# Expert weights in pair slots: 4 MB loads with 32 KB rows for gate and up, and the down biases moved to the last group

## What is computed

```python
def moe_ffn(h, w_router, b_router, w_e_gate, b_e_gate, w_e_up, b_e_up, w_e_down, b_e_down):
    ...
    def expert_step(acc, args):
        wg, bg, wu, bu, wd, bd, cw = args
        g = jnp.minimum(xt @ wg + bg, SWIGLU_LIMIT)
        u = jnp.clip(xt @ wu + bu, -SWIGLU_LIMIT, SWIGLU_LIMIT)
        y = ((u + 1.0) * g * jax.nn.sigmoid(SWIGLU_ALPHA * g)) @ wd + bd
        return acc + cw[:, None].astype(y.dtype) * y, None
```

## Time and profile before

| what | value |
|---|---|
| median of 3 runs | 1139.85 us |
| profiled execution, its own time | 1138.89 us |
| its span (first to last instruction) | 1137.1 us |
| TensorE matmul busy | 1092.3 us, 96% |
| VectorE, ScalarE, GpSimd busy | 409.6, 179.3, 90.3 us |
| share of the 16 DMA engines of the weights' queue | 93.1% of the span |
| moved | 438.88 MB, mean 386 GB/s |

### The profile page before, as it was taken

How to read it: one execution, slowest core, us unless ns; L and a number is a source line. 1 busy time by engine, 2 the same in 40 slices (tenths; PEclk the granted TensorE clock), 3 DMA queues, 4 the chain that set the end, 5 groups by cost and what they waited for, 6 DMA issues and landing times.

```text
span 1137.1 us, 14543 instructions
## 1 busy us (share of the span) xinstructions
PE 1092.3 (96%) x5733; PEld 513.9 (45%) x5733; DVE 409.6 (36%) x973; ACT 179.3 (16%) x370; POOL 90.3 (8%) x89
## 2 busy tenths in 40 slices
PE   8999999999999999999999999999999999999997
PEld 7888899843333333333333333333333333333333
DVE  5883666532223222223322222222222222222222
ACT  6546664400000000000000000000000000000000
POOL 2226447000000000000000000000000000000000
PEclk9999999999989999999999999999999999999999
DMA  9955724999999999999999999999999999999996
GB/s 309 344 195 220 225 75 147 425 405 421 428 418 412 427 429 428 427 429 428 429 428 429 428 429 427 429 428 429 429 428 429 426 429 427 430 427 428 426 428 280
DMA packets 50572, 438.88 MB, mean 386 GB/s; under 512 B 6786, under 2 KB 12998, under 8 KB 25062
## 3 DMA queue, kind: packets, MB, share of 16 engines
q1 hardware_dynamic: 50470, 438.23, 93.1%
q10 hardware_dynamic: 64, 0.14, 0.0%
HBM read 437.30 MB, written 1.05 MB: 385 GB/s over the span
## 4 chain that ended last, share of the span: by engine, by line
PE 65%; DMA 34%; issue 0%; DVE 0%; ACT 0%; POOL 0%; POOLq 0%; SPq 0%; DVEq 0%
PE bank L1939 35%; DMA ring<-in_w_e_up_dram 18%; DMA ring<-in_w_e_gate_dram 12%; PE bank L1912 3%; PE bank L1960 3%; DMA ring<-in_w_e_down_dram 3%; PE bank L1928 2%; PE bank L1533 2%; PE bank L1701 1%; PE bank L1702 1%; PE bank L1703 1%; PE bank L1980 1%; PE bank L1542 1%; PE bank L1544 1%; PE bank L1543 1%; PE bank L1536 1%
## 5 line engine op out<-in xcount | busy, mean ns | idle before, releaser
L1939 PE MATMUL bank<-ring,heads 128*64 128x512 f32 x3004 | 679.0, 599 | 14.8 <-DMA ring<-in_w_e_gate_dram 13.1
L1939 PEld LDWEIGHTS bank<-ring,heads 128*64 128x64 f32 x3004 | 204.2, 137 | 421.0 <-issue 376.5
L1463 DVE TENSOR_TENSOR x<-x,bank 128x512 f32<-128x512 f32 x124 | 79.8, 684 | 144.9 <-PE bank L1960 144.9
L1411 DVE TENSOR_SCALAR heads<-bank 128x512 f32<-128x512 f32 x32 | 22.1, 691 | 289.5 <-PE bank L1939 289.5
L907 ACT ACTIVATE work<-bank 128x256 f32<-128x256 f32 x32 | 12.3, 383 | 492.3 <-PE bank L1973 492.3
L708 POOL TENSOR_TENSOR x<-x,heads 128x256 f32<-128x256 f32 x2 | 1.4, 729 | 912.1 <-ACT heads L941 912.1
L1960 PE MATMUL bank<-heads,work 64*128 64x512 f32 x248 | 72.3, 641 | 0.0
L409 POOL TENSOR_TENSOR w_lo<-ring,w_hi 128x1024 fp32r<-128x1024 f32 (+1 forms) x35 | 65.3, 1894 | 53.8 <-ACT w_hi L731 53.8
L731 ACT ACTIVATE w_hi<-ring 128x512 fp32r<-128x512 f32 (+2 forms) x82 | 57.6, 732 | 25.2 <-PE bank L1790 7.3
L1912 PE MATMUL bank<-work,xn 128*128 128x128 f32 x480 | 58.5, 275 | 0.0
L1912 PEld LDWEIGHTS bank<-work,xn 128*128 128x128 f32 x480 | 56.0, 192 | 0.0
(11 more groups left out here) (323 smaller groups left out, 976.3 us busy)
## 6 DMA issues: line engine op xcount, KB each, us to landing
ring<-in_w_e_gate_dram SPq DMA_DIRECT2D x61, 2048.0 KB, 30.6
ring<-in_w_e_up_dram SPq DMA_DIRECT2D x61, 2048.0 KB, 31.7
ring<-in_w_e_down_dram SPq DMA_DIRECT2D x60, 2048.0 KB, 31.8
ring<-in_w_in_dram SPq DMA_DIRECT2D x8, 2048.0 KB, 10.2
ring<-in_w_e_down_dram SPq DMA_DIRECT2D x8, 1024.0 KB, 17.5
spare<-in_w_e_gate_dram SPq DMA_DIRECT2D x2, 2048.0 KB, 15.7
ring<-in_w_out_dram SPq DMA_DIRECT2D x2, 2048.0 KB, 8.1
ring<-in_w_e_up_dram SPq DMA_DIRECT2D x4, 1024.0 KB, 7.1
```

The source lines that it names most:

```text
L1411: nc.vector.tensor_scalar(e_g, banks[1][:, :], LIMIT, None, ALU.min).then_inc(g_made, 1)
L1463: ins = nc.vector.tensor_tensor(x[:, t, 512 * h:512 * h + 512], x[:, t, 512 * h:512 * h + 512], bank67[:, j % 2, :], ALU.add)
L1939: last = mm(bank[C * half:C * half + C, :], lhs(kk), kept_row[half] if kept else w[:, k, 512 * half:512 * half + 512], start=(kk == 0 and ...
```

## The change

- `ring` becomes four pair slots of 4 MB (`PAIR_ORDER`, `slots_of`); matrix n of the order takes pair n mod 4. The order of a step is gate(e), down(e - 1), up(e): `place_of` gives 3e - 1, 3e, 3e + 1.
- Gate and up weights are laid out so that partition p holds rows 8p to 8p + 7: as one load of 4 MB, 32 KB in one piece a partition (`load_matrix`). Halves of gate and up then are 16 KB pieces at a step of 32 KB. Down keeps its layout. `xn`, `gain_m` follow the new layout.
- Gate and up of experts 4 to 27 come by `load_matrix`, issued when the pair's last user is done as a whole; both halves of `product` wait for the whole. All else (experts 0 to 3, every down, the last group) comes by halves. In the loop the two halves of down are issued together.
- `spare` is filled by one load instead of two. The loads of the head and of experts 1 to 3 are written out in `first_experts`.
- TensorE: gate 0, gate 1, down 0, down 1, up 0, up 1. In even steps the gather stands before gate 0. The first scatter stands inside up 0, after its second k. VectorE's `keep_x` of even steps goes ahead of `keep_hT`.
- The down biases are no longer added at the step of expert 3, but in the last group: for column half 0 in the step of expert 28, for half 1 in that of expert 29 (`biased_half = u`).

The diff, cut to its core (the helpers that count semaphore values, `adds` and `count_at`, and the last expert's index changes are left out):

```diff
 RING = (3, 4, 5)
-EX_ORDER = (7, 3, 6, 4, 5, 0, 1, 2)
-EX_SLOTS = len(EX_ORDER)
...
+        def place_of(m, u):
+
+            return {"gate": 3 * u - 1, "up": 3 * u + 1, "down": 3 * u + 3}[m]
+        LAST_PLACE = {("up", STEPS - 1): 9, ("down", STEPS - 2): 10, ("down", STEPS - 1): 11}
+        def slots_of(n):
+            pair = PAIR_ORDER[n % len(PAIR_ORDER)]
+            return 2 * pair, 2 * pair + 1
+
...
                 src = a[ex_src[m]][0, bass.ds(e, 1)] if not isinstance(e, int) else a[ex_src[m]][0, e:e + 1]
-                return src.rearrange("o (h p k) n -> h p (o k n)", h=2, p=P)[h]
-
-            def load_half(m, h, e, place):
-
-                s = EX_ORDER[place % EX_SLOTS]
+                if m == "down":
+                    return src.rearrange("o (h p k) n -> h p (o k n)", h=2, p=P)[h]
...
+            def load_matrix(m, e, n):
+
+                s = slots_of(n)[0]
+                src = a[ex_src[m]][0, bass.ds(e, 1)].rearrange("o (p k) n -> p (o k n)", p=P)
+                sp.dma_start(ring[:, s:s + 2, :].rearrange("p s n -> p (s n)"), src).then_inc(ring_in[s], 16)
+
...
+            def first_experts():
+
+                def as_freed(m, e, of, done):
+
+                    for h in range(2):
+                        sp.wait_ge((half_done, mat_done)[h][of], done)
+                        load_half(m, h, e, place_of(m, e))
+                sp.wait_ge(*low_done(OUT))
+                load_half("gate", 1, 1, place_of("gate", 1))
+                sp.wait_ge(y_made, KD)
+                load_half("gate", 0, 0, 0)
+                sp.wait_ge(*low_done(OUT + 3))
+                sp.wait_ge(*low_done(OUT + 4))
+                load_half("up", 0, 0, place_of("up", 0))
+                sp.wait_ge(*low_done(OUT + 7))
+                sp.wait_ge(*low_done(OUT + 8))
+                load_half("up", 1, 0, place_of("up", 0))
+                load_by_halves()
+                load_half("gate", 0, 1, place_of("gate", 1))
+                for i in range(len(INTO_USED)):
+                    load_as_used(i)
+                sp.wait_ge(mat_done["up"], 1)
+                load_half("gate", 1, 2, place_of("gate", 2))
+                as_freed("down", 1, "gate", 2)
+                as_freed("up", 2, "down", 1)
+                as_freed("gate", 3, "up", 2)
+                as_freed("down", 2, "gate", 3)
+                as_freed("up", 3, "down", 2)
+
+            def expert_body(base, u, last=False):
+
+                it = base + u
+                ends = last and u == STEPS - 1
+                e = sp.snap(sp.to_reg(it & (E - 1)), min_val=0, max_val=E - 1)
+                e_before = sp.snap(sp.to_reg((it - 1) & (E - 1)), min_val=0, max_val=E - 1)
+                now, prev = sp.to_reg(it), sp.to_reg(it - 1)
+                if last:
+                    if u:
+                        for h in range(2):
+                            sp.wait_ge((half_done, mat_done)[h]["up"], prev)
+                            load_half("gate", h, e, place_of("gate", u))
+                    if ends:
+                        n = LAST_PLACE["up", u]
+                        s = slots_of(n)[1]
+                        sp.wait_ge(half_done["gate"], now)
+                        load_half("up", 0, E - 1, n)
+                        sp.wait_ge(mat_done["gate"], now)
+                        sp.dma_start(ring[:, s, 0:1024 * 3], source("up", 1, E - 1)[:, 0:1024 * 3]).then_inc(ring_in[s], 16)
+                        for h in range(2):
+                            sp.wait_ge((half_done, mat_done)[h]["down"], prev)
+                            load_half("down", h, e_before, LAST_PLACE["down", u - 1])
+                        return
+                    for h in range(2):
+                        sp.wait_ge((half_done, mat_done)[h]["gate"], now)
+                        load_half("down", h, e_before, place_of("down", u - 1))
+                    for h in range(2):
+                        sp.wait_ge((half_done, mat_done)[h]["down"], prev)
+                        load_half("up", h, e, place_of("up", u))
+                    return
+                sp.wait_ge(mat_done["up"], prev)
+                load_matrix("gate", e, place_of("gate", u))
+                sp.wait_ge(mat_done["gate"], now)
                 for h in range(2):
+                    load_half("down", h, e_before, place_of("down", u - 1))
+                sp.wait_ge(mat_done["down"], prev)
+                load_matrix("up", e, place_of("up", u))
...
@@ -1388,9 +1422,11 @@
                 rcols = rv[:, it:it + 4, :] if isinstance(it, int) else rv[:, bass.ds(it, 4), :]
                 chain(nc.vector.tensor_copy(now.rearrange("p (s j) -> p s j", j=4), rcols))
 
+                if not first and u % 2 == 0:
+                    keep_x(it, u)
                 if not first:
                     keep_hT(it)
-                if not first and not ends:
+                if u % 2 and not ends:
                     keep_x(it, u)
                 if u % 2 == 0:
                     for t in range(NT):
...
+            def product(m, h, bank, lhs, it, base, u, first=False, in_last=False, between=None):
+
+                n = 0 if first and m == "gate" else place_of(m, u)
+                if in_last:
+                    n = LAST_PLACE.get((m, u), n)
...
+                    s = slots_of(n)[h]
+                    halves = isinstance(base, int) or m == "down" or in_last
+                    by = h if halves else 0
+                    pe.wait_ge(ring_in[slots_of(n)[by]], count_at(n, by, base, in_last))
                     w = ring[:, s, :].rearrange("p (k n) -> p k n", k=4)
                 if h == 0 and m != "down" and not (first and m == "gate"):
...
+                    if between and k == 2:
+                        between()
...
+            def scatter(i, t, biased_half=None):
+
+                if biased_half == 0 and t == 0:
...
                         pe.wait_ge(added, i * 2 + h + 1)
+                    biases = h == biased_half
                     if biases:
...
             def expert(base, u, in_last=False):
 
                 it = base + u
+                biased_half = u if in_last else None
                 if u % 2 == 0:
                     pe.wait_ge(ex_made, it - 1)
+                    gather(None, 1, False)
                 pe.wait_ge(g_made, it)
                 product("gate", 0, banks[1], x_of(u), it, base, u, False, in_last)
                 turn_h(it)
-                if u % 2 == 0:
-                    gather(None, 1, False)
-                elif u % 2:
+                if u % 2:
                     gather(it + 3, 0, True)
                 turn_hot(it)
+                if u % 2 == 0:
+                    pe.wait_ge(ex_made, it)
+                product("gate", 1, banks[1], x_of(u), it, base, u, False, in_last)
                 pe.wait_ge(ehT_made, it)
                 product("down", 0, banks[3], h_of, it - 1, base, u - 1, False, in_last)
                 product("down", 1, banks[3], h_of, it - 1, base, u - 1, False, in_last)
-                if u % 2 == 0:
-                    pe.wait_ge(ex_made, it)
-                product("gate", 1, banks[1], x_of(u), it, base, u, False, in_last)
-                scatter(it - 1, 0, isinstance(it, int) and it == 3)
-                product("up", 0, banks[2], x_of(u), it, base, u, False, in_last)
-                scatter(it - 1, 1, isinstance(it, int) and it == 3)
+                product("up", 0, banks[2], x_of(u), it, base, u, False, in_last,
+                        lambda: scatter(it - 1, 0, biased_half))
+                scatter(it - 1, 1, biased_half)
                 product("up", 1, banks[2], x_of(u), it, base, u, False, in_last)
 
```

More of the change, by code:

```diff
@@ L414, in wait_block, with adds, count_at @@
             eng.wait_ge(ring_in[s], v)
[L417 to L432, removed]
+        def place_of(m, u):
+            return {"gate": 3 * u - 1, "up": 3 * u + 1, "down": 3 * u + 3}[m]
+        LAST_PLACE = {("up", STEPS - 1): 9, ("down", STEPS - 2): 10, ("down", STEPS - 1): 11}
+        BY_HALVES = 11
+        def slots_of(n):
+            pair = PAIR_ORDER[n % len(PAIR_ORDER)]
+            return 2 * pair, 2 * pair + 1
+        def adds(n):
+            if n == place_of("down", 0):
+                return 32, 32
+            return 16, 16 if n < BY_HALVES or n % 3 == 0 else 0
+        PER_GROUP = (48, 16)
+        def count_at(n, h, base, in_last=False):
+            if isinstance(base, int):
+                return n_in[slots_of(n)[h]] + sum(adds(i)[h] for i in range(n % 4, n + 1, 4))
+            until = BY_HALVES - 1 if in_last else n + 3 * STEPS
+            landed = n_in[slots_of(n)[h]] + sum(adds(i)[h] for i in range(n % 4, until + 1, 4)) - PER_GROUP[h]
+            if in_last:
+                landed += 16 * (n // 4 + 1)
+            return landed + base * (PER_GROUP[h] // STEPS)
+        FIRST_USED = [("gate", 0), ("up", 0), ("gate", 1)]
+        INTO_USED = [("up", 0, 1), ("gate", 0, 2), ("up", 1, 1)]
```

(18 more changed lines are left out.)

106 lines of the change are left out of this document (35 added, 71 removed).

## The result

The changed kernel takes 1145.59 us (median of 5 executions, 1145.03 to 1147.8), the kernel before 1139.57 beside it. The ratio is 1.0056, 95% interval 1.0044 to 1.0067: slower by 6.0 us, where 7.2 were forecast. The profiled execution took 1145.03 us, span 1143.3, against 1138.89 and 1137.1 for the kernel before: 6.1 and 6.2 us more.

A forecast was written before the change was run, and what follows sets the result against it. The weight stream decides before the last group; inside it TensorE is within 2 us of deciding. 6.0 + 6.3 - 2.0 - 1.9 + 1.7 - 3.4 + 0.5 = +7.2 us, on the median 1147.0 us, range 1141 to 1153.

The forecast's parts named there:

- Up of expert 27 handed over whole, +6.0: Handover to the last group: up of expert 27 waits for its whole 4 MB and takes in the first scatter, +6.0 us.
- Biases, +6.3: Last group, experts 28 and 29: added bias products and lost scatter overlap on TensorE, +6.3 us, bounds 4.2 and 8.4.
- Waits of the last group, -2.0: Last group: with TensorE late by over 10 us, its three short waits for loads go, -2.0 us.
- The dip, -1.9: Expert 3, near 334 us: without biases there, the stream's dip to 408 and 411 GB/s goes, -1.9 us.
- the thin queue, +0.5: Early loads, expert 4's gate: the pair goes out later, which thins the queue, +0.5 us, bounds 0 and 1.9.
- 32 KB rows, -3.4: 48 pair loads, experts 4 to 27: 128 fewer rows each save 0.072 us, -3.4 us; bound 0 if engines split rows.
- The clock, +1.7: TensorE at the biased steps and the wait before up of expert 27: one clock fall, +1.7 us, bounds 0 and 5.1.
- Order: New TensorE order: down after gate half 1, scatter inside up; put at nothing, else up to 2 us in the last group.
- The rival with the stream as the bound to the end: Last group: late up and biases are absorbed by the stream, only -4.8 us remains, 1135 us; chance 8%.
- That the long loads bring nothing: Loop loads: longer rows no faster or disturbing each other, part 4 is 0 or +2, 1150.4 to 1152.4 us; chance 20%.
- That pieces at a step of 32 KB are slower: Halves of experts 1 to 3 and 29 to 31: slower 16 KB pieces hurt the early stretch, 1153 us; chance 5%.
- That the clock falls at every chance: Two biased steps and the wait before up of expert 27: 5.1 us for 1.7, 1150.4 us; chance 13%.

The follow-up runs named there:

- the kernel with both: Changed kernel with experts 24 to 27 loaded by halves and the down biases at experts 24 and 25, bias product first: 1136.43 us, 0.9967; repeated 1136.47 us, 0.9977.

## Why the prediction was right

The sign and the mechanism held: the stream decides up to expert 27, TensorE from there, and the change loads both the handover and TensorE's part. Step by step:

- **Up of expert 27 handed over whole, +6.0.** With the terms of the stream the prediction has it start at 1005.85 and end at 1015.57; it started at 1006.14 and ended at 1016.01. Aligned, it is within 0.3 us. Undone in the last loop group, it gives 3.1 to 4.3 us and not 6.0. Of the 6.0 only 4.9 are the second half's load; 1.06 are the first scatter, which now stands behind the wait and stays there by halves too, and eight long loads fewer cost 0.6. That leaves 4.3, and the aligned trace has 4.1. In the kernel with both, 0.3 to 0.8 us of the last group's waits come back as well.
- **Biases, +6.3.** 6.30 by the timelines, 6.6 by leaving them out. The step of half 1 loses its overlap, as taken: 2.1 us.
- **Waits of the last group, -2.0.** None is left.
- **The dip, -1.9, and the thin queue, +0.5.** The dip is gone and no new one came: 425 and 436 GB/s. In the kernel with all by halves, where these two are all that acts on the stream, half 0 of up of expert 27 begins 1.2 us earlier than before, aligned; the prediction has 1.4. In the three edits of the kernel before that take the biases from expert 3 it begins, aligned, 1.2, 1.8 and 1.0 us earlier. The medians of two of them show only 0.4 and 0.0 us, so what of it reaches the end stays open. What the term did not say is that in the changed kernel the same delay would cost 4.1.
- **32 KB rows, -3.4.** 3.9 by the traces. The size came out nearly right, but the term was scaled from a stretch of 6 us with 4 KB rows, and the runs do not show that the rows are the cause and not the 48 loads fewer. The packets speak against rows split at 16 KB, the condition of its bound 0: 43387 against 50300 with all by halves, 144 fewer for each of the 48 loads. That engines disturb each other with longer rows no run shows (431 against 428 GB/s).
- **The clock, +1.7.** The term is taken from expert 3 of the kernel before: granted clock 0.51, and 16 matmuls in 4.88 and 5.35 us for 3.65, 1.2 and 1.7 us, which with the 6.3 are the 9 us that TensorE is late there. It failed for the change. In the last group the clock did not fall before TensorE's last product ended at 1138.4 us, not even after the steps of 3.15 us of half-filled products; up of expert 27 waited only 0.57 us. It fell eight times in the loop instead. From 480 to 977 us the timeline has eleven waits of 2.2 us; after eight of them (509 to 977 us) the eight matmuls behind take 2.9 to 3.6 us, after three (480, 685, 889) they take 1.94. After the nine shorter waits, of up to 1.0 us, it never fell. A fall costs some 1.6 us (the next wait is that much shorter), with which an expert needs 26.9 + 1.6 = 28.5 us, an estimate, while the stream needs 29.2 (509.43 to 538.65), so none costs anything: the next up only waits 0.6 us in place of 2.2. Of the 17 ups from 509 to 977 us eight run at the low clock in their first matmuls, and none of it reaches the end. There is chance in this. It fell at expert 26, so expert 27 had the short wait; it did so in four of the five traces with pairs to the end, and in the fifth, where expert 27 waited 2.83 us, no fall followed. And the fall that the term meant does happen: in the kernel before with the biases last it came behind just such a step of 3.15 us and cost 1.7 us. In what share of the executions was not measured.
- **Order.** Two experts without biases take 53.84 us in the new order (1039.42 to 1093.26), 53.54 before: 0.15 us an expert, and the start of expert 0 is 0.5 us later in this trace. The prediction had the order at nothing but the scatter behind the wait, which it priced in the handover.

Sum on the profiled execution: up of expert 27 ends 1.6 us later (predicted 1.2), and behind it lie 6.3 - 2.0 + 0.3 = 4.6 us (predicted 6.3 - 2.0 + 1.7 = 6.0); the 0.3 is what is left over, of the size of the order. That is 6.2 against 7.2. The mis-sized term is the clock.

The rival with the stream as the bound to the end is out: less work for TensorE gives 6.6 us in the kernel after. That the long loads bring nothing is out by 428 against 431 GB/s and 3.9 us. That pieces at a step of 32 KB are slower is out by the 428 GB/s of the kernel with all by halves. That the clock falls at every chance is out for this execution: it fell at none of the three places that the prediction had priced.

What stays open: how much of the dip reaches the end of the kernel before; whether longer rows or fewer loads make the rate; whether pairs or the new order make a late expert 3 so dear; and the start of expert 0, which begins 1.3 to 1.9 us later in some profiled executions (228.17 to 228.97 in four of the kernels above), where the gather ahead of it takes 3.3 to 3.65 us for 2.02. In which share of the executions this happens was not measured, and it is as large as some of the effects looked for.

## What to carry to other kernels

Price a coarser transfer where the pacing resource hands over to the other one, not in the loop, where it is free: here 48 long loads gained 3.9 us and the last of them gave over 4 back. Long loads in the loop and halves in the last loop group have both. Work that must be added somewhere goes where its engine has slack and enough is queued behind it, neither into the tail nor at the start of a queue that is still thin: at experts 24 and 25 the biases cost 6.1 us less than in the tail (halves in that group), and 3.0 less than at expert 3 (pairs).

## What the runs showed of the hardware that was not expected

- Queued loads gained little from being longer: 428 GB/s with loads of 2 MB and rows of 16 KB, 431 where two thirds of the bytes come in loads of 4 MB with rows of 32 KB; pieces of 16 KB at a step of 32 KB ran at 428 too.
- A wait of 2.2 us between full stretches of products was followed by a fall of the granted clock eight times in eleven, some 1.6 us each; over the eight traces with 4 MB loads for both gate and up in the loop it is 61 times in 78. One of 2.83 us, at 1008.05 in the kernel with whole pairs and the biases at 24, was not. With up by halves all seven waits of 2.3 to 4.2 us were followed by a fall and the three of 1.5 to 1.7 us were not; no shorter wait was, in any of these traces from 366 us on. So the length of a wait alone does not tell what the clock will do.
- 4.2 us of products on 32 and 64 rows were followed by a fall twice in the kernel before (granted clock 0.51 and 0.50 behind them) and not at all in the kernel with the biases at expert 3 (1.00); steps of 3.15 us once in the kernel before with the biases last (0.50) and not in the kernel after (1.00). So these products alone do not decide it either.
- Two products side by side on different rows took 1.06 us for four pieces (1095.48 to 1096.54 in the kernel after). With another product between them they had no overlap: 1.05 us for each pair of pieces (1064.38, 1065.43, 1066.48, end 1067.53).
